# Row factors of the first attention's probabilities on GpSimd instead of VectorE

## The reference

```
idx_score = sum over 8 heads of relu(qi @ ki^T) * wi          # causal; each query keeps its 256 best keys
s = qd @ k_d[sel]^T * 64**-0.5;  p = softmax(s);  o_dsa = p @ v_d[sel]
s = qg @ k^T * 64**-0.5 (causal); p = softmax(s);  o_slc, o_win = p @ v
o_nsa = o_cmp * gate[0] + o_slc * gate[1] + o_win * gate[2]
out   = concat(o_dsa, o_nsa) @ w_out
```

## Time and profile before

| what | value |
|---|---|
| median of 3 runs | 4299.42 us (4298.96 to 4314.07) |
| the profiled execution's own time | 4277.35 us |
| its span in the profile | 4275.5 us |
| busy: TensorE, VectorE, ScalarE, GpSimd | 83%, 51%, 21%, 31% of the span |
| TensorE's granted clock, mean of the execution | 0.911 |
| the first attention | from about 262 to 545 us of the span |

### The profile page before, as it was taken

The page is one execution under the profiler, slowest core; times in us unless marked ns, Lnnn a source line. Parts: engine busy times, 40 slices in busy tenths (PEclk is TensorE's granted clock), DMA queues, the critical chain, the costliest instruction groups (busy, mean ns, idle before and its releaser), DMA issues.

```text
span 4275.5 us, 33127 instructions
## 1 busy us (share of the span) xinstructions
PE 3543.1 (83%) x10814; PEld 1818.0 (43%) x10814; DVE 2175.2 (51%) x4744; ACT 910.9 (21%) x1890; POOL 1332.9 (31%) x1241
## 2 busy tenths in 40 slices
PE   8368998999998989979999974768676878776877
PEld 4244544444454565546544564334232323232323
DVE  0567524421004466756525448864687876433443
ACT  1224412000023124622111312111121212111111
POOL 0200000000000005600001013453777777777775
PEclk9667999999999999979899987889988998899999
DMA  3010021343221212211212356774999999999997
GB/s 149 13 50 1 1 99 66 141 158 136 80 79 47 82 59 74 89 54 60 89 59 79 130 188 217 254 254 173 384 344 351 349 370 364 360 371 372 357 373 284
DMA packets 171914, 765.17 MB, mean 179 GB/s; under 512 B 19256, under 2 KB 19256, under 8 KB 160224
## 3 DMA queue, kind: packets, MB, share of 16 engines
q0 software_dynamic: 157904, 580.06, 36.9%
q1 hardware_dynamic: 13824, 182.97, 11.4%
q10 hardware_dynamic: 16, 0.02, 0.0%
HBM read 744.08 MB, written 18.89 MB: 178 GB/s over the span
## 4 chain that ended last, share of the span: by engine, by line
PE 51%; DVE 15%; issue 9%; POOL 6%; DMA 4%; ACT 3%; another core or an unknown queue 1%; POOLq 0%; DVEq 0%; ACTq 0%
PE ps L252 14%; PE ps L258 12%; POOL arena L2742 6%; PE ps L1406 6%; DVE arena L2772 5%; PE ps L1336 5%; PE ps L2695 5%; DMA arena<-in_pu,arena 3%; PE ps L1712 2%; PE ps L220 2%; DMA arena<-in_pv,arena 1%; PE ps L1699 1%; PE ps L786 1%; PE ps L2320 1%
## 5 line engine op out<-in xcount | busy, mean ns | idle before, releaser
L2695 PE MATMUL ps<-arena 128*128 128x512 f32 x2048 | 1024.1, 649 | 369.7 <-issue 158.6
L2772 DVE CUSTOM_DVE_ANT_0 arena<-arena 128x1024 f32<-128x1024 f32 x512 | 623.5, 1222 | 406.7 <-DMA arena<-in_pu,arena 374.1
L2695 PEld LDWEIGHTS ps<-arena 128*128 128x128 f32 x2048 | 400.3, 205 | 974.2 <-issue 765.6
L252 PE MATMUL ps<-arena 128*128 128x512 f32 (+1 forms) x1768 | 757.7, 589 | 33.2 <-ACT arena L2261 24.4
L2742 POOL DMA_INDIRECT arena<-in_pu,arena x512 | 563.9, 1101 | 406.0 <-issue 95.2
L2742 POOL DMA_INDIRECT arena<-in_pv,arena x512 | 553.7, 1081 | 196.1 <-issue 128.6
L258 PE MATMUL ps<-arena 128*128 128x512 f32 (+2 forms) x1408 | 529.0, 536 | 3.1 <-DVE arena L1253 0.9
L252 PEld LDWEIGHTS ps<-arena 128*128 128x128 f32 x1768 | 338.4, 193 | 438.3 <-issue 433.6
L258 PEld LDWEIGHTS ps<-arena 128*128 128x128 f32 x1408 | 267.2, 190 | 261.1 <-issue 216.9
L263 POOL TENSOR_TENSOR arena<-arena 128x1 f32<-128x1 f32 (+7 forms) x38 | 61.4, 1618 | 997.1 <-DVE arena L630 430.0
L220 PE MATMUL ps<-arena 128*128 128x128 f32 x1046 | 198.8, 327 | 199.0 <-ACT arena L812 49.8
(11 more groups left out here) (342 smaller groups left out, 3332.7 us busy)
## 6 DMA issues: line engine op xcount, KB each, us to landing
arena<-in_w_in SPq DMA_DIRECT2D x27, 2048.0 KB, 8.9
arena<-in_w_ada SPq DMA_DIRECT2D x12, 2048.0 KB, 7.9
arena<-in_w_ff_in SPq DMA_DIRECT2D x8, 2048.0 KB, 12.3
arena<-in_w_ff_out SPq DMA_DIRECT2D x8, 2048.0 KB, 12.4
arena<-in_w_pq SPq DMA_DIRECT2D x8, 2048.0 KB, 8.3
aside<-arena POOLq DMA_DIRECT2D x20, 512.0 KB, 4.7
arena<-in_w_at SPq DMA_DIRECT2D x4, 2048.0 KB, 8.0
arena<-in_w_o SPq DMA_DIRECT2D x4, 2048.0 KB, 8.2
```

What stands on the lines that cost most here:

```text
L252: x = t.matmul(PS[:, b, 0:n], hT[:, k, i * 128:(i + 1) * 128], w[:, k, :], start=k == 0, stop=k == nk - 1)
L2695: x = t.matmul(PS[:, b + c, :], DG[n % 4], row(f)[:, 512 * c:512 * c + 512], start=j == 0, stop=j == 127)
L2772: v.tensor_tensor_reduce(row(f), row(f), TT[i], 1.0, 0.0, ALU.mult, ALU.add, DOT[i % 2][:, j:j + 1]).then_inc(*pe.V.step("dot", 128 * i + j))
```

## The change

VectorE no longer multiplies the probabilities. It still computes the factor, whose last small instruction now carries the name `gain`. GpSimd gets a loop of its own, `attn_gpsimd`: for group j-1 it waits for `gain`, multiplies the two heads' tiles in place and counts `scaled` on its own line. TensorE waits for that line. The memory part of GpSimd is advanced by one step an iteration from iteration 23 on, in place of being run alone.

```diff
@@ -1011,7 +1011,7 @@
                     if 0 <= j - 2 < NG:
                         i = j - 2
                         x = probs(i, h)
-                        t.wait_ge(*at1.V.at("scaled", i, h))
+                        t.wait_ge(*at1.G.at("scaled", i, h))
                         b = bank(t, (3,), at1.A, "pt", i, h)
                         for a in range(GROUPS[i][0] + 1):
                             y = turned(t, PS[:, b, 128 * a:128 * a + 128], x[:, 128 * a:128 * a + 128])
@@ -1061,6 +1061,19 @@
                 hook(j)
             drain(memory, 100)
 
+        def attn_gpsimd(g):
+            memory = memory_gpsimd(g)
+            for j in range(NG + 1):
+                if j > 0:
+                    i = j - 1
+                    r = RWG[i % 4]
+                    for h in range(2):
+                        g.wait_ge(*at1.V.at("gain", i))
+                        g.tensor_scalar(probs(i, h), probs(i, h), r[:, 6 + h:7 + h], None, ALU.mult).then_inc(*at1.G.step("scaled", i, h))
+                if j >= 23:
+                    drain(memory, 1)
+            drain(memory, 100)
+
         def attn_vector(v):
             wait_all(v, cm.A, cm.P, cm.V, lt.P, lt.A)
             drain(before_vector(v, 0), 100)
@@ -1084,13 +1097,10 @@
                     qt, p, br = GROUPS[i]
                     r = RWG[i % 4]
                     v.wait_ge(*at1.A.at("exp", i, 1))
-                    v.reciprocal(r[:, 6:8], r[:, 4:6]).then_inc(*at1.V.step())
+                    v.reciprocal(r[:, 6:8], r[:, 4:6]).then_inc(*at1.V.step("gain", i))
                     if br:
                         gate = GT[:, qt, :].rearrange("p (h b) -> p b h", b=3)[:, br, 2 * p:2 * p + 2]
-                        at1.V.own(v).tensor_tensor(r[:, 6:8], r[:, 6:8], gate, ALU.mult).then_inc(*at1.V.step())
-                    at1.V.own(v)
-                    for h in range(2):
-                        v.tensor_scalar(probs(i, h), probs(i, h), r[:, 6 + h:7 + h], None, ALU.mult).then_inc(*at1.V.step("scaled", i, h))
+                        at1.V.own(v).tensor_tensor(r[:, 6:8], r[:, 6:8], gate, ALU.mult).then_inc(*at1.V.step("gain", i))
                 hook(j)
             drain(memory, 100)
 
@@ -2896,7 +2906,7 @@
             latent_gpsimd(g)
             compress_gpsimd(g)
             memory_load(g)
-            drain(memory_gpsimd(g), 100)
+            attn_gpsimd(g)
             pn_gpsimd(g, ow)
             xattn_gpsimd(g)
             pn_gpsimd(g, xo)
```

## The result

Over 20 runs of each the median is 4292.74 us (4274.99 to 4308.76) with the change and 4306.93 us (4290.78 to 4327.0) without it; the ratio is 0.9964, 95% interval [0.9949, 0.9979]. The change makes the kernel faster, by 14.2 us on the medians. That is clear of zero, but smaller than the 0.5% (21.5 us) that the prediction took as what one measurement can tell from no change.

A forecast was written before the change was run, and what follows sets the result against it. VectorE was taken to set the pace in 23 attention iterations: 4.2 + 4.6 + 6.3 = 15.1 us, less 1.5 for the clock, 13.6 off the median 4299.42 gives 4285.8 us; range 4267 to 4303.

The forecast's parts named there:

- A: Likeliest case: VectorE's path shortens in the first attention, 4285.8 us, own range 4283 to 4290; chance 0.60.
- the three paced stretches: Attention iterations 2 to 9, 15 to 21 and 26 to 33, where VectorE sets the pace: 4.2, 4.6 and 6.3 us saved.
- correction for the clock: Third selection stretch: 2.5 of 8 iterations at TensorE's low clock gain 0.19 us, not 0.79; 1.5 us less saving.
- Bounds by the nearest rows: GpSimd's multiplication of 512 columns priced from a cast and a two-input sum: 0.48 to 1.17 us, about 0.6 taken.
- the next step: Is GpSimd hidden in the last stretch: one multiplication under 2.2 us, two under 3.8, so up to 1.9 each.
- B: Shared port: five iterations with VectorE's weighted sums give back GpSimd's multiplications, 1.9 to 11.2 us saving remain; chance 0.15.
- C: Denser work brings TensorE's high clock earlier, mainly in the 27 us before the second selection: saving 24.6, 4275; chance 0.13.
- D: GpSimd becomes the bound in the last stretch, from 2.15 us per 512-column multiplication; 4323 us at 4.5; chance 0.05.
- E: No change at the end: TensorE with its waits for ScalarE sets the pace once VectorE is quicker, 4299; chance 0.07.

The follow-up runs named there:

- e5: The change plus three VectorE instructions of 512 columns behind the factor in iterations 44 to 46; GpSimd's pair took 4.13 us beside products, 3.60 beside copies, 3.11 beside maxima.
- the run with the first three tiles: The change, but GpSimd multiplies only for the first three query tiles and VectorE for the last; the groups took 255.47 us, ratio to before 0.9953.
- e9: The change with the factor also computed on GpSimd for the first three tiles and all GpSimd multiplications in two-operation form; groups 254.54 us, ratio to before 0.9959.

## Why the prediction was right

**The saving.** Forecast 13.6 us, ratio 0.9968; measured 14.5 us in the attention, 14.2 and 0.9964 on the medians. The forecast time, 4285.8 us, was 6.9 too low, and 4292.74 lies outside A's own 4283 to 4290: over 20 runs the kernel before has a median of 4306.93 and not the 4299.42 of the three runs from which I subtracted. The step that did the work, counting VectorE's distance only in the iterations in which L1079 does not wait, holds: the three paced stretches give 13.1 us against 13.6 forecast, and the last tile gives nothing. That the total came as near as it did is in part luck, as 1.35 us arose where the sum had nothing and the correction for the clock came to its size by another way (below).

**By stretch.** The first was counted as 8 x 0.52 = 4.2 us and gave 3.72, for the step from group 2 to 3 is set by TensorE now; that it has nothing to do with GpSimd the run without multiplication shows (3.80 there). The second was counted as 4.6 and gave 4.34, the difference being L955 beside GpSimd. For the third the sum had 6.3 - 1.5 = 4.8, and 5.07 came.

**The correction for the low clock** has about the right size, 1.2 in place of 1.5 us, for another reason than the one given. By the sum 2.5 of the eight iterations fall on the low clock and gain 0.19 us each. The trace has no such iteration: the seven steps from group 26 to 33 gain 0.72 to 0.79 us each, and no score pass in them waits for TensorE. In this execution the clock was at its high level in the first six of them, but that is not the reason. In the kernel with the added VectorE instructions (e5) the step from group 28 to 29 was granted 0.53 and still took 6.00 us, not the 6.80 that TensorE needs for a group at the low level, and TensorE was busy for 4.94 of it. TensorE is a group ahead in these iterations, which would explain why one slow group does not hold VectorE up; the sum had taken the 6.80 us as a period. What was lost, was lost in the one step from group 33 to 34. It took 5.66 us in place of 5.37, where the sum had a gain, and TensorE was busy for all of it at a clock of 0.81. This step varied from 4.58 to 7.00 us between the kernels, and the granted clock of the stretch from 0.83 to 0.93.

**What was counted at nothing.** Groups 0 to 2 and 22 to 26 brought 0.35 and 1.0; the second goes with the granted clock, by which groups 22 to 26 took 18.35 to 21.48 us in the ten kernels without VectorE's multiplications there, at 0.98 to 0.82, and 20.7 and 20.6 in the two with them, at 0.85 and 0.86.

**The mis-sized term** is GpSimd's multiplication. "Bounds by the nearest rows" gave 0.48 to 1.17 us for 512 columns and I took 0.6; it is 1.56 undisturbed and 1.64 on the average. The nearest row, a cast, was the wrong guide, and even the sum of two inputs did not bound it. Nothing came of it, because the next step asked for the limit and not for the price: up to 1.9 us, and the disturbed pair of the port experiment (4.13 us, 0.10 us lost) puts it at about 2. The Trainium skill (GPSIMD Engine Reference, "Engine selection") has one-input work near line rate on GpSimd. VectorE's multiplication of 512 columns took 0.49 us here; GpSimd's took 1.56 with one operation and 0.69 with two, both undisturbed, so only the second form comes near to it.

**The rivals.** B, contention on VectorE, costs 0.4 us in the change and 1.1 in the run with the first three tiles (0.09 in groups 2 to 10, 0.50 in 15 to 22, 0.54 in 26 to 33, each against the run without multiplications). The two engines do disturb each other, and in the change it is mostly GpSimd that pays: its pair with 384 columns takes 2.47 us alone (397.50) and 4.03 beside L735 and three weighted sums (385.31), while the L920 with 512 columns went from 0.751 to 0.773 us. But who pays is not fixed. Here is the same pair, for group 26, in the change and then in the run with the first three tiles:

```profile
390.05 3.98 POOL L1072 TENSOR_SCALAR arena<-arena 128x384 f32<-128x384 f32 x2 [0.71 <-DVE arena L1103]
...
390.53 1.66 DVE L920 SCALAR_TENSOR_TENSOR arena<-arena 128x512 f32<-128x512 f32 x2
...
392.22 0.69 DVE L929 TENSOR_TENSOR arena<-arena 128x512 f32<-128x512 f32 x1
```

```profile
391.04 3.44 POOL L1072 TENSOR_SCALAR arena<-arena 128x384 f32<-128x384 f32 x2 [0.71 <-DVE arena L1103]
...
391.53 1.93 DVE L920 SCALAR_TENSOR_TENSOR arena<-arena 128x512 f32<-128x512 f32 x2
...
393.49 0.87 DVE L929 TENSOR_TENSOR arena<-arena 128x512 f32<-128x512 f32 x1
```

In the second GpSimd is 0.54 us quicker and VectorE 0.45 slower, in a step that VectorE sets. GpSimd and VectorE run the same instructions there in both kernels; why it went the other way is not shown. The prediction had looked at L920 only; L929 and L955, also with two SBUF inputs, are where VectorE paid (L929 in the step from group 15 to 16 too, 0.81 in place of 0.56).

The Trainium skill (SBUF — State Buffer, "Who interferes with whom") has the second to start block fully until the first is done. In the probe GpSimd lost 1.0 us of the 2.3 during which VectorE used two inputs, and VectorE 0.24, so neither stood still for the whole of the other's work. The exemption that the Trainium skill makes there for instructions with one SBUF input, outside the two-port modes, agrees for row maxima (3.11 us) and for `max` and `match_replace` (unchanged at 0.697 and 0.677 us); the copies, also with one SBUF input, did cost GpSimd 0.5 us.

C, an earlier high clock in groups 10 to 15, did not occur: 25.48 us at 0.50 as before. D exists: it sets in at some 1.3 times the actual price (4.0 us for a pair against 3.1), and at twice the price it has taken back the gain (ratio 1.0017). E is excluded: the attention became 14.49 us shorter.

**Open** stays why groups 22 to 26 get 0.82 to 0.98 of the clock in executions whose work on TensorE is the same, and so whether the 1.0 us there belongs to the change. One execution of each kernel can't tell.

## What to carry to other kernels

Before moving work to a slower engine, mark the iterations in which the giving engine really sets the pace (its first instruction does not wait) and count the distance to the next start only there: 23 of 48 iterations carried 13.1 of the 14.5 us. Where the other engine works a group ahead, the time that it needs for one slow group is not the period. For the receiving engine ask for the latest moment at which its result is wanted, not for its price; a price that was wrong by 2.6 times did no harm here because the limit stood at 1.9 us. If a multiplication by a per-row factor on GpSimd comes near such a limit, write it with a second operation: here that was 0.69 in place of 1.56 us.

## What was unexpected of the hardware

- GpSimd's multiplication of a tile by a per-row factor takes 0.61, 0.92, 1.24 and 1.56 us undisturbed for 128, 256, 384 and 512 columns, 2.5 ns a column; with a second multiplication in the same instruction, by the constant 1.0, it takes 0.37, 0.47, 0.58 and 0.69 us, 0.8 ns a column. With a second per-row factor in place of the constant it took 0.45, 0.56 and 0.67 us for the first three (e9).
- A row maximum on VectorE leaves GpSimd alone; three products of two SBUF tiles cost GpSimd's pair 1.0 us and three copies 0.5. In the paced stretches the same meeting cost VectorE 0.0 us in one kernel and 0.45 in another.
- The reciprocal of two columns costs VectorE's chain 0.07 us, though its row shows 0.16.
